# Byte positions of the split weight parts against the moving operands in a 2-layer hybrid decoder step

## The reference, cut to what matters

```python
h = rmsnorm(x, norm1_g) * (1 + sc1) + sh1
z = h @ w_in                                  # 1024 x 3340
...                                           # three head groups: HGRN2, RG-LRU, gated DeltaNet
x = x + gt1 * (concatenated @ w_out)
h = rmsnorm(x, norm2_g) * (1 + sc2) + sh2
...                                           # PEER: scores, top 16 of 128 x 128 keys, per head
act = gelu(einsum(u[idx], h)) ; x = x + gt2 * einsum(gw * act, v[idx])
```

## Time and profile before

| | |
|---|---|
| median of 3 runs | 2373.42 us (2370.58 to 2381.35) |
| the profiled execution, its own time | 2368.92 us |
| its span | 2366.9 us |
| PE, PEld | busy 96% and 88% of the span |
| DVE, ACT, POOL | 63%, 54%, 45% |
| mean granted TensorE clock | 0.97 |
| split products: ps_u, ps_y, ps_z | 6144, 6144 and 1296 matmuls |

### The profile page before, as it was taken

One profiled execution on the slowest core, in us unless ns is written; L12 is line 12 of the kernel. 1 busy time (PEld: TensorE's weight loads), 2 busy tenths in 40 slices (PEclk: granted clock), 3 DMA queues, 4 the chain that ended last, 5 costly groups with the idle time before them and its releaser, 6 DMA issues. The chain is left out here.

```text
span 2366.9 us, 58299 instructions
## 1 busy us (share of the span) xinstructions
PE 2266.2 (96%) x20478; PEld 2076.5 (88%) x20478; DVE 1494.1 (63%) x3095; ACT 1268.8 (54%) x2439; POOL 1054.6 (45%) x960
## 2 busy tenths in 40 slices
PE   6989999999999999999999799999999999999998
PEld 4955869999998799999989367799999978999997
DVE  3746636963225968888666664299432288787885
ACT  3533215567557955555556322165665587555554
POOL 0010106884446746566300210088644475665661
PEclk8978999999999999999999779999999999999999
DMA  7475034555552079899545821455555502898992
GB/s 281 155 280 201 3 131 164 178 181 202 188 189 92 6 264 312 287 301 312 194 171 170 310 101 38 137 185 178 199 183 187 188 33 91 295 312 275 312 312 100
DMA packets 123806, 455.40 MB, mean 192 GB/s; under 512 B 13744, under 2 KB 14256, under 8 KB 122544
## 3 DMA queue, kind: packets, MB, share of 16 engines
q1 hardware_dynamic: 105264, 386.80, 45.9%
q0 software_dynamic: 18432, 67.12, 10.3%
HBM read 449.37 MB, written 4.49 MB: 192 GB/s over the span
## 5 line engine op out<-in xcount | busy, mean ns | idle before, releaser
L426 POOL TENSOR_TENSOR parts<-ring,parts 128x512 fp32r<-128x512 f32 x358 | 463.9, 1298 | 472.0 <-ACT parts L419 457.6
L419 ACT ACTIVATE parts<-ring 128x512 fp32r<-128x512 f32 x620 | 389.2, 632 | 348.4 <-PE ps_u L473 280.5
L469 PE MATMUL ps_u<-h_parts,parts 128*128 128x256 f32 x4096 | 563.5, 280 | 0.9 <-ACT parts L419 0.6
L2649 PE MATMUL ps_y<-act_parts,parts 128*128 128x256 f32 x4096 | 563.0, 279 | 0.0
L469 PEld LDWEIGHTS ps_u<-h_parts,parts 128*128 128x128 f32 x4096 | 514.4, 188 | 3.1 <-ACT parts L419 1.7
L2649 PEld LDWEIGHTS ps_y<-act_parts,parts 128*128 128x128 f32 x4096 | 515.1, 188 | 0.7 <-ACT parts L2589 0.3
L426 DVE TENSOR_TENSOR parts<-ring,parts 128x512 fp32r<-128x512 f32 x262 | 180.6, 692 | 372.8 <-ACT parts L419 351.1
L2698 POOL TENSOR_TENSOR act_parts<-big,act_parts 128x256 fp32r<-128x256 f32 x256 | 246.5, 963 | 304.4 <-ACT act_parts L2678 304.4
L473 PE MATMUL ps_u<-h_parts,parts 128*128 128x256 f32 x2048 | 322.7, 279 | 1.4 <-DVE parts L426 1.1
L2653 PE MATMUL ps_y<-act_parts,parts 128*128 128x256 f32 x2048 | 322.3, 279 | 0.0
L473 PEld LDWEIGHTS ps_u<-h_parts,parts 128*128 128x128 f32 x2048 | 275.2, 188 | 2.2 <-DVE parts L426 1.5
(11 more groups left out here) (398 smaller groups left out, 2813.1 us busy)
## 6 DMA issues: line engine op xcount, KB each, us to landing
ring<-in_stream SPq DMA_DIRECT2D x522, 512.0 KB, 3.4
more_ring<-in_stream SPq DMA_DIRECT2D x126, 512.0 KB, 4.9
extra_ring<-in_stream SPq DMA_DIRECT2D x48, 512.0 KB, 5.8
big<-in_stream SPq DMA_DIRECT2D x16, 512.0 KB, 11.7
out_state_out<-big SPq DMA_DIRECT2D x2, 1440.0 KB, 7.0
big<-in_state SPq DMA_DIRECT2D x2, 1280.0 KB, 10.1
big<-in_mixc SPq DMA_DIRECT2D x2, 1024.0 KB, 7.7
big<-in_spots SPq DMA_DIRECT2D x2, 1024.0 KB, 5.5
```

Source lines behind the costliest of these rows:

```text
L419: eng.activation(m.parts[:, q % PARTS, 0, :], half_tile(m, t, half), ACT.Copy).then_inc(s["hi_ready"], 1)
L426: eng.tensor_tensor(m.parts[:, q % PARTS, 1, :], half_tile(m, t, half), m.parts[:, q % PARTS, 0, :].bitcast(F32), ALU.subtract).then_inc(m ...
L469: pe.matmul(out, hi[:, k, :], hr[:, side, kk, 0:tokens], start=(kk + side == 0), stop=False)
L2649: pe.matmul(ps[:, half * KD // 2 + k, :], hi[:, k, :], act_parts[:, j % AHEAD, side, :], start=False, stop=False)
```

## The change

The buffer gain (576 bytes) is taken right behind ring, ahead of parts, and a new buffer line_end of 32 bytes, which nothing reads or writes, is taken behind small. No instruction is added, removed or reordered; only addresses differ.

```diff
         self.x = sb("x_res", [P, KD, NT])
         self.ring = sb("ring", [P, RING, D])
+        self.gain = sb("gain", [P, 2, KD, 1 + NB])
         self.parts = sb("parts", [P, PARTS, 2, D // 2], F32R)
         self.keep = sb("keep", [P, KEEP_W])
         self.small = sb("small", [P, SMALL_W])
+        self.line_end = sb("line_end", [P, 8])
         self.mod = sb("mod", [P, 6 * KD, 1 + NB])
-        self.gain = sb("gain", [P, 2, KD, 1 + NB])
         self.cond = sb("cond", [P, KD, COND])
```

## The result

The changed kernel takes 2404.65 us (median of 4 runs, 2400.7 to 2407.84) against 2372.0 us before (4 runs): a ratio of 1.0141, 95% interval 1.0114 to 1.0168. It is slower by 27 to 40 us. The profiled execution took 2407.84 us; its span and engine rows answer to the earlier trace rows.

What follows compares the result with a forecast made beforehand. PE's matmul pitch in the split stretches was taken as the bound; ps_u and ps_y gave 35 us less, all else nothing, so 2368.9 us became 2334, or 2338 against the median; range 2305 to 2405 us.

Steps and rivals of the forecast that it cites:

- What bounds the kernel: In the six split stretches of ps_z, ps_u and ps_y, 70% of the time, only PE's matmul pitch counts.
- Does it hang on addresses: An identical split matmul costs up to 7 ns more or less by where its operand lies, cheapest at -96.
- No effect: Rival, chance 0.22: the 7 ns are a fixed price beside the weight load; time stays 2373 us (2362 to 2385).
- The term of ps_u and ps_y: Moving these 12288 matmuls from distance 32 to 0 saves 2.9 ns each, 35 us less.
- a straight line between -96 (293.3) and 32 (296.3): From ps_z durations, gives 0.75 ns at distance 0 for ps_u and ps_y, 9 us: the next-to-nothing reading.
- middle of the two upper readings: For ps_u and ps_y, 2.9 ns less, between 5 ns (conflict wholly gone) and 0.75 ns (the line).
- The bounds: For ps_u and ps_y: best 5 ns less a matmul, 61 us; worst 4.3 ns more, 53 us.
- ps_z: Its 1296 matmuls trade four distances for four as evenly spread: 0, between 6 us less and 3 us more.
- The rival "slower": Chance 0.28: at distance 0 ps_u and ps_y streams meet in memory; up to 53 us more (2426), half 2400 us.
- POOL: Next late in the first 51 u tiles; costed at nothing, as a rival 7 us less gained, 2345 us.
- gain's move: No instruction more or less; the norms only read and write gain at another address.
- the splitting engines: Source starts shift when parts moves, worth 3 ns on DVE, which has slack: nothing.

Runs made afterwards that it cites:

- e1: Kernel before with 480-byte pads ahead of h_parts and act_parts, putting ps_u and ps_y at distance 0; gain and parts unmoved: 2401.37 us against 2371.92, ratio 1.0129.
- e2: Kernel before with 480-byte pads ahead of h_parts and act_parts plus 32 bytes ahead of parts: distance 0, operands off multiples of 64 bytes; 2405.63 us, single run.
- e11: Kernel before with 160-byte pads ahead of h_parts and act_parts, putting ps_u and ps_y at distance 192: 2343.93 us against 2371.9, ratio 0.9886.
- e12: Changed kernel with pads of 8 floats ahead of h_parts and act_parts, returning ps_u and ps_y to distance 32: 2376.96 us, ratio 1.0014 to before.
- e8: Kernel before with ps_u at distance 0, its high-part matmuls done as 4 of 512 columns instead of 8 of 256, ps_y at distance 240: 2365.48 us.

## Why the prediction was wrong

- **What bounds the kernel** held: PE's pitch in the split stretches. The stretches moved with the pitch, in every run.
- **Does it hang on addresses** held in kind: the distance between the two operands counts, and neither operand's place by itself (e1, e2). "No effect" is out: the same instruction starts every 113.3 to 120.0 ns, with nothing edited but addresses. The Trainium skill, "SBUF — State Buffer", section "Who interferes with whom", calls PE's read port for the moving operand and the one for weight loads independent; these traces don't agree, since the distance between the two operands changes the pitch. The Trainium skill, "TensorE: Matmul & The Clock Gate", section "Back-to-back issue gap", gives 109.2 ns for a lone warm matmul of 256 columns; no distance reached that in these streams.
- **The term of ps_u and ps_y is the step that failed**, in size and in sign: forecast 2.9 ns less, measured 3.1 ns (ps_u) and 3.3 ns (ps_y) more. Half of its working was "a straight line between -96 (293.3) and 32 (296.3)", where 296.3 is the mean over the distances 32, 160 and 288, and there is no line: the price jumps within 16 bytes (192 and 208, 0 and 16). The reading under it, that k = 3 was cheap because of its distance, was not a reading of the distance alone either: in after the high part's k = 3, at 384, was the dearest (310 and 313 ns) and the low part's k = 3, at 384 too, lasted 294 at most. The likely reason is that the neighbours of other distances set the rhythm; no run isolates it. The "middle of the two upper readings" then put a number between two readings of the same sign; the worst bound, 4.3 ns more, stood beside them and was left out of the middle.
- **The bounds held.** The best was put at 5 ns less; the best rhythm found is 3.4 ns under 116.7 (113.3). The worst was put at 4.3 ns; 3.3 is the dearest mean seen in these stages.
- **ps_z**: 0 forecast, with 6 less to 3 more; measured 2.5 ns more a matmul, 3.3 us. A miss just past its bound.
- **The rival "slower"** is what happened: its point of decision was +1 ns, the pitch came to +3.3, and its half price gave 2400 us against 2404.65 measured. The place and the sign were right, and its chance, 0.28, was low; the "half" had no reading behind it, so that the time came so near is luck. Its mechanism (both streams in the same stretch of memory at the same moment) isn't shown: 96 costs 120.0 ns as well, where the two starts lie 96 bytes apart. The row held against it, ps_g with both operands at distance 0 and no loss, is of another kind of product: plain float32, 128 columns in 112 ns, about half as many columns a ns. ps_w, plain float32 too (242 ns a record for 288 columns), kept its median of 406 ns in after.
- **POOL**: it doesn't bind at a half of 1.36 us (e11), so the cost of nothing was right. The change itself didn't test it, since it slowed PE: after, five low halves cover 7.06 us.
- **gain's move, the splitting engines**: nothing, as told (e12).
- **Why the medians lie nearer** (32.65 us) than the profiled executions (38.9 us): the pitches make 43 us (40 + 3), about the 42.3 by which the stretches grew, and the rest shrank by 3.3. Two stretches outside the split ones, before and then after, are 4.6 us shorter together (all others 1.3 longer):

```profile
738.90:827.90 89.00, 84.62 (x579) 67.14 (x580) 81.15 (x130) 81.50 (x132) 67.14 (x65) 0.95 0.01 2
1295.10:1535.20 240.10, 214.81 (x2602) 150.94 (x2602) 114.68 (x306) 65.98 (x156) 26.03 (x39) 0.89 0.41 150
...
751.80:838.80 87.00, 81.31 (x570) 65.54 (x580) 80.47 (x130) 80.67 (x131) 67.03 (x65) 0.98 0.00 1
1316.80:1554.30 237.50, 211.86 (x2602) 148.50 (x2602) 115.27 (x306) 65.40 (x156) 25.64 (x39) 0.90 0.43 152
```

They are shorter where the granted clock is higher (0.98 against 0.95, 0.90 against 0.89). Over the 17 runs of before the time goes with the mean granted clock too, from 2365.9 us at 0.973 to 2379.1 at 0.964, with 0.968 in the middle; the four runs of after had 0.972 to 0.974. A higher granted clock in after's runs would make the difference of the medians smaller; how much of it this is, no run shows. The rhythms of distance 32 add little: e12's 72 more tiles at 2827 ns are 2 us.

## What to carry to other kernels

Where a run of matmuls each with its own weight load is the bound, the distance of the moving operand from the weights, modulo 256 or 512 bytes, is a tuning knob worth some 3% of the pitch either way (113.3 and 120.0 ns around 116.7), and it costs a pad. Equal alignment of the two is no safe choice: distance 0 was among the dearest here. Don't interpolate between distances, and don't carry a value over to matmuls of another width (e8, ps_z); try several pads and look at the pitch, which a single profile shows to the nanosecond, and test the chosen one in several runs, since a distance may allow more than one rhythm.

## What the runs showed of the hardware that was not expected

- Float32r matmuls of 256 columns, each beside the weight load of the next, at most distances lock into exact rhythms: 113.3, 116.7, 117.8, 118.3, 119.2 or 120.0 ns, constant over dozens to hundreds of tiles. One execution can hold two of them at one distance: 113.3 and 117.8 at 192 or 448, 116.7 and 117.8 at 32 in ps_u.
- At the distances 0, 96 and 256 a matmul of 256 columns costs 288 cycles of 2.4 GHz (120.0 ns), 32 over its columns. e8 didn't confirm that this is one cycle for each 16 bytes of a weight block's 512.
- Weight loads share the loss: 192 ns in place of 188 in the mean at distance 0.
